# One stationary for w and the decayed q in the gated delta layer, and the next block's q and k scaled ahead of this block's output

## The reference

```python
q = l2norm(heads(q, DK_A)) * (DK_A ** -0.5)
k = l2norm(heads(k, DK_A))
...
qg = q * jnp.exp(gc)[..., None]                 # decayed q
kg = k * jnp.exp(gc[..., -1:] - gc)[..., None]
def step(S, inp):                               # S is 128 x 128 per head
    qg_c, kg_c, u_c, w_c, attn_c, gl_c = inp
    v_new = u_c - jnp.einsum('bhck,bhkv->bhcv', w_c, S)
    o = jnp.einsum('bhck,bhkv->bhcv', qg_c, S) + jnp.einsum('bhij,bhjv->bhiv', attn_c, v_new)
    S = S * gl_c[..., None, None] + jnp.einsum('bhck,bhcv->bhkv', kg_c, v_new)
    return S, o
...
o = rmsnorm(o, g_norm) ; o = o * jax.nn.silu(z)
```

## Time and profile before

| | us |
|---|---|
| median of 3 runs | 4349.92 (4340.74, 4349.92, 4349.94) |
| the profiled execution, its own time | 4347.94 |
| its span | 4346.2 |
| PE busy in the span | 3972.3 (91%) |
| DVE, ACT, POOL busy | 2370.6 (55%), 1386.5 (32%), 843.3 (19%) |

### The profile page before, as it was taken

How to read it: one execution, slowest core, us unless ns; L and a number is a source line. 1 busy time by engine, 2 the same in 40 slices (tenths; PEclk the granted TensorE clock), 3 DMA queues, 4 the chain that set the end, 5 groups by cost and what they waited for, 6 DMA issues and landing times. The chain is left out here.

```text
span 4346.2 us, 58235 instructions
## 1 busy us (share of the span) xinstructions
PE 3972.3 (91%) x22955; PEld 2621.1 (60%) x22955; DVE 2370.6 (55%) x4650; ACT 1386.5 (32%) x2924; POOL 843.3 (19%) x544
## 2 busy tenths in 40 slices
PE   8999999996999999997899999997999999899877
PEld 4555555553455454555888888886656565565544
DVE  4566556652233333332556566662256676778875
ACT  1222222221111111111333333332244454565552
POOL 0344334432122211121222222220000000000000
PEclk9999999997999999998999999996999999999998
DMA  6343334234011110014000000012010100000000
GB/s 245 128 141 112 136 127 141 103 121 150 26 36 36 36 32 27 30 36 151 25 24 23 26 26 26 16 63 79 30 35 18 34 18 23 30 18 18 18 13 17
DMA packets 139772, 259.86 MB, mean 60 GB/s; under 512 B 17205, under 2 KB 64650, under 8 KB 139402
## 3 DMA queue, kind: packets, MB, share of 16 engines
q1 hardware_dynamic: 139530, 256.46, 17.0%
HBM read 217.11 MB, written 39.33 MB: 59 GB/s over the span
## 5 line engine op out<-in xcount | busy, mean ns | idle before, releaser
L459 PE MATMUL e_ps<-arena 128*128 128x386 f32 x1792 | 611.6, 492 | 17.8 <-DVE e_hh L716 7.0
L1082 PE MATMUL o_ps<-arena,o_xT 128*128 128x512 f32 x1280 | 564.4, 594 | 0.8 <-ACT o_xT L1190 0.8
L459 PEld LDWEIGHTS e_ps<-arena 128*128 128x128 f32 x1792 | 331.1, 191 | 249.1 <-issue 32.8
L1082 PEld LDWEIGHTS o_ps<-arena,o_xT 128*128 128x128 f32 x1280 | 239.2, 191 | 279.0 <-issue 278.9
L1612 PE MATMUL d_ps<-hT_in,arena 128*128 128x128 f32 x3072 | 393.3, 283 | 13.4 <-ACT hT_in L1798 11.4
L1612 PEld LDWEIGHTS d_ps<-hT_in,arena 128*128 128x128 f32 x3072 | 360.4, 193 | 29.0 <-ACT hT_in L1798 12.6
L2402 PE MATMUL s_ps<-hT_in,arena 128*128 128x128 f32 x2160 | 257.3, 279 | 6.7 <-PEq L67 6.7
L2402 PEld LDWEIGHTS s_ps<-hT_in,arena 128*128 128x128 f32 x2160 | 253.7, 196 | 10.1 <-issue 9.1
L1171 PE MATMUL o_ps<-o_w_out,o_gt 128*128 128x512 f32 x512 | 225.2, 598 | 4.6 <-ACT o_gt L1247 4.6
L2526 PE MATMUL s_ps<-arena 128*128 128x512 f32 x512 | 228.3, 600 | 0.0
L560 PE MATMUL e_ps<-e_w_out,e_gt 128*128 128x512 f32 x512 | 225.0, 598 | 0.0
(11 more groups left out here) (458 smaller groups left out, 6626.2 us busy)
## 6 DMA issues: line engine op xcount, KB each, us to landing
arena<-l_w_in SPq DMA_DIRECT2D x32, 1040.0 KB, 8.5
xb<-x SPq DMA_DIRECT2D x64, 512.0 KB, 3.4
arena<-l_w_in SPq DMA_DIRECT2D x16, 1544.0 KB, 8.7
arena<-l_w_in SPq DMA_DIRECT2D x16, 1024.0 KB, 8.6
arena<-l_w_in SPq DMA_DIRECT2D x32, 504.0 KB, 7.1
o_scratch<-w_ada SPq DMA_DIRECT2D x16, 768.0 KB
arena<-l_w_in SPq DMA_DIRECT2D x5, 2048.0 KB, 18.9
arena<-w_in SPq DMA_DIRECT2D x5, 2048.0 KB, 14.1
```

Of the source, the lines that this page charges most:

```text
L459: m = pe.matmul(bank[(g + k) % 2][:, 0:N], rows[:, kk * P:(kk + 1) * P], cols[:, kk, :], start=(kk == 0 and k in (0, 1, 4)), stop=(kk == 3 ...
L1082: m = pe.matmul(bank[c % 2][:], xT[:, k * P:(k + 1) * P], W_in[:, k, off:off + 512], start=(k == 0), stop=(k == KT - 1))
```

## The change

1. w transposed and the decayed q of a chunk go into one buffer `wq`, side by side: 64 columns of w and 64 of q for each head. One matmul per head and chunk (four in place of eight per chunk) multiplies S by both. In chunk 0 w has columns 0 to 63, in chunk 1 it has columns 64 to 127, so that w times S lies at the chunk's own rows; the decayed q times S lies at the other half. Chunk 0 goes to bank 7, chunk 1 to bank 2.
2. The output is therefore spread over two banks, with the halves of the partitions exchanged. attn times `vnew` goes there, ScalarE squares it with two instructions of 64 rows, DVE scales it with eight instructions of 64 rows (four before, of 128), the gate z is copied from its bank with the halves exchanged (two instructions of 64 rows for each part, and one for the small columns), and SP stores it with two DMAs.
3. Bank 2 is also where the inverse's products go, so TensorE's wait for the output of the turn before stands in front of the inverse now.
4. On TensorE one piece of filling comes between the first chunk's product and its update, where the product with q stood, and one less behind `turn_qk` (two, not three).
5. On DVE the scaling of q and k of block j stands in front of the output of block i, not behind it.
6. POOL scales q turned with two instructions of half the size. ScalarE waits for `gz` before it copies a new z.

The diff, cut to its core:

```diff
-        qgT = qn
-        wT = sb("wT", [P, 4, P])
+        wq = sb("wq", [P, 2, 4, P])
 ...                                     # sync
-                sp.dma_start(oa_out[bass.ds(b.i * P, P), :], oa[:]).then_inc(oa_stored.sem, 16)
+                for a in (0, DC):
+                    sp.dma_start(oa_out[bass.ds(b.i * P + a, DC), :], oa[DC - a:P - a, :]).then_inc(oa_stored.sem, 16)
 ...                                     # tensor
                 pe.wait_ge(*R_ready.upto(i))
+
+                pe.wait_ge(*oa_ready.before(i))
 ...
-                pe.wait_ge(*oa_ready.before(i))
                 for n in range(2):
 ...
                     for h in range(4):
-                        m = pe.matmul(bank[2][a:a + 64, h * P:(h + 1) * P], wT[:, h, a:a + 64], S[:, h, :], start=True, stop=True)
+                        m = pe.matmul(bank[(7, 2)[n]][:, h * P:(h + 1) * P], wq[:, n, h, :], S[:, h, :],
+                                      start=(h == 0), stop=False, skip_group_check=True)
                     m.then_inc(*wS_made.inc())
-
-                    for h in range(4):
-                        pe.matmul(bank[7][a:a + 64, h * P:(h + 1) * P], qgT[:, h, a:a + 64], S[:, h, :],
-                                  start=(h == 0), stop=False, skip_group_check=True)
+                    if n == 0:
+                        fill()
                     if n and not b.last:
                         turn_v(j)
 ...
                 for h, a in tiles:
-                    m = pe.matmul(bank[7][a:a + DC, h * P:(h + 1) * P], attn[a:a + DC, h, :], vnew[a:a + DC, h, :], start=False,
-                                  stop=True, skip_group_check=True)
+                    m = pe.matmul(bank[2 if a else 7][DC - a:P - a, h * P:(h + 1) * P], attn[a:a + DC, h, :], vnew[a:a + DC, h, :],
+                                  start=False, stop=True, skip_group_check=True)
                 m.then_inc(*o_made.inc())
                 if not b.last:
                     turn_qk(j)
-                    fill(3)
+                    fill(2)
 ...                                     # scalar
-                act.activation(osq[:], by_head[7], ACT.Square).then_inc(*osq_ready.inc())
+                act.activation(osq[DC:P], by_head[7][DC:P], ACT.Square).then_inc(*o.inc())
+                act.activation(osq[0:DC], by_head[2][0:DC], ACT.Square).then_inc(*osq_ready.inc())
 ...
                 if not b.last2:
+                    act.wait_ge(*gz_ready.upto(i))
                     project(b.i + 2, p, 3)
 ...                                     # vector
                 if not b.last:
                     sums_qk(j)
+                    normalise_qk(j)
                 dve.wait_ge(*ro_ready.upto(i))
                 dve.wait_ge(*gz_ready.upto(i))
 
-                dve.wait_ge(oa_stored.sem, 16 * i + 1)
-                for h in range(4):
-                    dve.scalar_tensor_tensor(oa[:, h * P:(h + 1) * P], by_head[7][:, h, :], ro[:, h:h + 1], gz[:, h, :],
-                                             ALU.mult, ALU.mult).then_inc(*(oa_ready if h == 3 else o).inc())
+                dve.wait_ge(oa_stored.sem, 32 * i + 1)
+                for n, a in ((7, DC), (2, 0)):
+                    for h in range(4):
+                        dve.scalar_tensor_tensor(oa[a:a + DC, h * P:(h + 1) * P], by_head[n][a:a + DC, h, :], ro[a:a + DC, h:h + 1],
+                                                 gz[a:a + DC, h, :], ALU.mult, ALU.mult)\
+                           .then_inc(*(oa_ready if n == 2 and h == 3 else o).inc())
                 if not b.last:
-                    for stage in (normalise_qk, copy_kT, mask_products):
+                    for stage in (copy_kT, mask_products):
                         stage(j)
 ...                                     # gpsimd
-                pool.tensor_tensor(qgT[:], qT[:], eG[:], ALU.mult).then_inc(*qg_ready.inc())
+                pool.tensor_tensor(wq[:, 0, :, DC:P], qT[:, :, 0:DC], eG[:, :, 0:DC], ALU.mult).then_inc(*o.inc())
+                pool.tensor_tensor(wq[:, 1, :, 0:DC], qT[:, :, DC:P], eG[:, :, DC:P], ALU.mult).then_inc(*qg_ready.inc())
```

More of the change, by code:

```diff
@@ L1575, in body @@
                 sp.wait_ge(*oa_ready.upto(b.i))
-                sp.dma_start(oa_out[bass.ds(b.i * P, P), :], oa[:]).then_inc(oa_stored.sem, 16)
+                for a in (0, DC):
+                    sp.dma_start(oa_out[bass.ds(b.i * P + a, DC), :], oa[DC - a:P - a, :]).then_inc(oa_stored.sem, 16)
             over_pipeline(sp, body)
-            sp.wait_ge(oa_stored.sem, 16 * BLOCKS + 1)
+            sp.wait_ge(oa_stored.sem, 32 * BLOCKS + 1)
             sp.wait_ge(h_stored.sem, 16 * BLOCKS + 1)
@@ L1804, in project @@
                 else:
-                    act.activation(zba[:, p, (c - 3) * ZH:(c - 2) * ZH], bank[c % 2][:, 0:ZH], ACT.Copy).then_inc(*proj_ready.inc())
+                    n = ZH if c == 3 else 512 - ZH
+                    for a in (0, DC):
+                        act.activation(zba[DC - a:P - a, p, (c - 3) * ZH:(c - 3) * ZH + n], bank[c % 2][a:a + DC, 0:n], ACT.Copy)\
+                           .then_inc(*(proj_ready if c == 3 and a else o).inc())
+                    if c == 4:
+                        act.activation(ba[:, p, :], bank[c % 2][:, n:ZH], ACT.Copy).then_inc(*proj_ready.inc())
             def softplus(i, p):
@@ L1933, in body @@
                 act.wait_ge(*wu_made.upto(i))
-                act.activation(wT[:, :, 0:DC], by_chunk[2], ACT.Copy).then_inc(*wT_ready.inc())
-                act.activation(wT[:, :, DC:P], by_chunk[5], ACT.Copy).then_inc(*wT_ready.inc())
+                act.activation(wq[:, 0, :, 0:DC], by_chunk[2], ACT.Copy).then_inc(*wT_ready.inc())
+                act.activation(wq[:, 1, :, DC:P], by_chunk[5], ACT.Copy).then_inc(*wT_ready.inc())
                 act.activation(u[:], by_head[3], ACT.Copy).then_inc(*u_ready.inc())
@@ L2101, in body @@
                     dve.wait_ge(*wS_made.upto(i, n + 1))
-                    dve.tensor_tensor(vnew[a:a + 64], u[a:a + 64], by_head[2][a:a + 64], ALU.subtract).then_inc(*vnew_ready.inc())
+                    dve.tensor_tensor(vnew[a:a + 64], u[a:a + 64], by_head[(7, 2)[n]][a:a + 64], ALU.subtract).then_inc(*vnew_ready.inc())
                     if not b.last:
```

## The result

| | us |
|---|---|
| before, median of 6 | 4348.99 (4340.74 to 4350.14) |
| after, median of 6 | 4366.67 (4365.66 to 4370.70) |
| ratio | 1.0048, 95% interval 1.0038 to 1.0059 |
| after, the profiled execution: its own time, its span | 4370.70, 4368.9 |

The change makes the kernel slower: 0.48% by the ratio of the runs, 17.7 us (0.41%) between the medians. The two measures differ by less than the width of the interval. The forecast was 4362 (range 4349 to 4380, slower with 0.68).

A forecast was written before the change was run, and what follows sets the result against it. Bound: nearly TensorE's own work, with a chain through DVE and ScalarE ending each turn. 14 turns x 0.8 = 11.2, -1.4, +0.4, clock +2.4: +12.6 on 4347.94 gives 4360.5, median 1.98 higher; forecast 4362, range 4349 to 4380.

The forecast's parts named there:

- turn 14: Turn without filling: -0.77 and -0.54 for update waits, -0.3 of L2036, 0.2 of output uncovered; -1.4 us.
- turn 15: Last turn, no filling: -1.54, then at the open end +0.49 squares, +1.14 output, +0.34 second DMA issue; +0.4 us.
- a term of 0.27: On TensorE, `turn_qk` comes 0.27 us later than before, since one more piece stands in front of it.
- three turns pay 0.8 each: Key products L1666 in slow-clock stretches: 3 turns, from an open 0 to 14, lose some 0.8 us each; +2.4.
- my own sign: Check on the changed trace: forecast right for another reason if the clock is 0.50 in more than half the turns.
- The clock falls in every turn: Rival: all 14 turns lose 0.8 to 2 us to the slow clock, in place of 2.4 altogether; 4371 to 4388; chance 0.13.
- my own case: The forecast's case: 0.45 to 1.15 us a turn and 0 to 6 slow-clock turns, 4354 to 4371; chance 0.60.
- term of 0.2 for changes of half: DVE's output: 0.11 us per change between halves of the rows, twice; output ends at 17.67, not 17.46.
- The rival of cheap instructions on 64 rows: At L2129 on DVE: from 0.15 us each a turn is 0.3 shorter, 4344; even at 0.18 to 0.20; chance 0.19.
- The rival of TensorE's work as the bound: TensorE's saving stays: a turn loses 1.5 us, 14 turns 21, time 4328; chance 0.06.

The follow-up runs named there:

- experiment 1: The changed kernel with k turned copied between the two halves of the output's eight DVE instructions; median 4346.18 us, ratio 0.9997 to the kernel before.
- experiment 6: The kernel before with only the output cut into eight instructions of 64 rows, in the old order; median 4364.59 us, ratio 1.0046.
- experiment 3: The changed kernel with filling as before: no piece behind the first chunk's product, three behind `turn_qk`; median 4351.94 us, ratio 1.0011 to the kernel before.
- experiment 4: The changed kernel with eight unread matmuls ahead of turning q and k and eight ahead of the key products; 4359.30 us, ratio 1.0028 to before.
- experiment 10: The kernel before without the inverse's first filling piece, ScalarE's copy of the third four projection pieces moved behind the squares; 4332.33 us, ratio 0.9966.
- 7: The changed kernel with output split about the copy of k, three pieces behind `turn_qk`, inverse's first piece dropped; 4331.51 us, ratio 0.9965 to before.
- experiment 5: The kernel before with q and k scaled ahead of the output, and ScalarE waiting for `gz` before copying z; 4345.93 us, ratio 0.9997.
- experiment 2: The changed kernel with the output again ahead of scaling q and k on DVE; median 4389.44 us, ratio 1.0098 to the kernel before.

## Why the prediction was right

By its own steps, with t = 0 at the first product (2613.58):

| step | forecast | measured |
|---|---|---|
| joint product, start to start of the next | 0.96 | 0.89 (before 0.93) |
| update 1, product 2 | 2.94, 5.78 | 2.77, 5.72 |
| wait for `vnew`, second chunk | 0.42 | 0.42 |
| `turn_qk` | 9.85 | 9.73 |
| L1657 turns the scaled q, wait | 15.48, 1.2 | 15.42, 1.09 |
| eight of L2129 | 2.2 to 2.4 | 2.32 |
| copy of k turned | 17.67 | 17.65 |
| wait in front of L1666 | 1.7 to 1.9 | 1.86 |
| a turn at the full clock | 58.4 (+0.8) | 58.28 (+0.69) |
| turns 0 to 13, slow clock | +2.4 | +10.3 |
| turn 14 | -1.4 | +2.5 |
| turn 15 | +0.4 | +1.3 |
| sum in the layer, profile on profile | +10.2 +2.4 = +12.6 | +20.0, of it -3.7 ahead of turn 0 |

**The mechanism held, step by step.** The place (the output's eight instructions ahead of the copy of k) is shown by experiment 1, which takes them away from there and gets 1.03 a turn back, and its price by experiment 6: 1.14 for cutting the output alone (there ahead of the scaling, so not the same place). Experiment 3 adds what my sum had as a term of 0.27 only: a piece left behind `turn_qk` would have hidden enough to make the turn shorter than before.

**The clock is the term that was mis-sized,** by a factor of four. I let three turns pay 0.8 each. Nine slow stretches fell into the 14 turns, and eleven turns are longer than 58.28. One stretch costs 10.3 / 9 = 1.1. The products take some 0.6 more (2633.62 - 2631.95 = 1.67 in the turn shown, 1.09 in experiment 4). The piece of L1617 behind them takes 1.0 more, all of it under the wait for `T`. And a wait of 0.3 to 0.55 for the copies of z comes in front of the turning of h (L1598, 2.9 us over 7 turns), at the start of turns that follow a slow piece. I had set that wait at 0, and in the turns at the full clock it is. My reason for three, that the idle stretch is shorter than the one in turn 14, was no reason: all 14 turns have 4.1 us with 1.1 busy there, and in nine of them the clock went to 0.50. By my own sign (over half of the turns at 0.50) the forecast is in part right for another reason. At the full clock the 14 turns would cost 9.7, which alone lies only just over 0.2%. "The clock falls in every turn", which I gave 0.13, is closer to what came than the three turns of my sum. In the changed kernel's profile the loss is about half chain and half clock. The Trainium skill ("TensorE: Matmul & The Clock Gate", section "HAM oscillation — how this bites in real kernels") describes a loop in which a wait for data in every turn makes every turn start at the slow clock. The trace agrees in kind: most turns run their products slow, behind a wait. But no slow stretch begins in five turns with the same waits, so such waits do not always bring it.

**Turn 14 was wrong in sign.** It takes 2.5 more, where I had 1.4 less. Over the kernels above it takes anything from 51.6 to 58.0; the slow stretches fall at other places in each, and no run separates its parts, so the cause stays open. **Turn 15** was sized low at its open end: the output 1.20 longer (2.32 against 1.12, forecast 1.14), the squares 0.61 (3032.18 - 3031.57, forecast 0.49), and the two DMA issues 0.75 (forecast 0.34):

```profile
3036.51 1.09 SPq L1576 DMA_DIRECT2D oa<-d_oa  x2
```

This is the counterpart of the last row. Together 2.56, of which 1.3 remain; by subtraction the rest saved some 1.3, where I had 1.54 for the updates. Both kernels run turn 15 at 0.50 from end to end.

**Ahead of turn 0** 3.7 us were gained that the forecast doesn't have. 1.0 of it comes from layers that are not touched. The other 2.7 came with a shorter stretch at the half clock (3.4 us, before 6.8) where the first blocks are prepared. The seven traces of kernels with the joint product all have the 3.4, and 85.5 to 85.7 us up to the first `T`; the five without it have the 6.8, and 88.2 to 88.4. So this is the change's doing, but by which of its parts, and that the shorter slow stretch is what gains it, was not tested.

**Luck in the total.** The forecast added 12.6 us; turns 0 to 15 took 23.8 more between the two profiles (the slow clock 7.9 above its term, turns 14 and 15 together 4.8, the full-clock turns 1.5 below theirs). That 4362 lies only 5 from 4366.67 is owed in part to the 3.7 gained ahead of turn 0, which I had not seen; the profiled execution of after is also the longest of its six, so that the medians are 5 us closer than the profiles. The bounds of my own case, 4354 to 4371, come out at 4355 and 4370 by their terms; nothing hangs on it.

**The held instruction.** The term of 0.2 for changes of half came out at 0.17 (2631.23 - 2628.98 = 2.25, less the 2 x 1.04 of the earlier trace rows). The rival of cheap instructions on 64 rows falls by the mean of one, taken from the groups of the output in experiment 10 (128 rows) and in 7 (64 rows):

```profile
L2121 DVE SCALAR_TENSOR_TENSOR d_oa<-d_ps,d_ro,d_gz 128x128 f32<-128x128 f32 x56 | 15.8, 344 | 7.0 <-ACT d_ro L1950 7.0
```
```profile
L2130 DVE SCALAR_TENSOR_TENSOR d_oa<-d_ps,d_ro,d_gz 64x128 f32<-64x128 f32 x112 | 32.0, 348 | 0.9
```

344 ns and 348 ns. The rival of TensorE's work as the bound falls too: some 2 us of work went (1.97 by the earlier trace rows, 2.3 between 7 and 10), and the turn became longer.

## What to carry to other kernels

Whoever joins two matmuls should count first what the readers of the joint result pay: half the rows cost DVE the same (348 ns against 344 ns here), so a result laid over two halves doubles each reader, and the order on that engine decides whether this lies in a chain. Work taken off an engine that waits in a chain comes back as waits, and when two of these stand close together the clock may fall as well (in 9 of 14 turns here, in none of experiment 6). Filling should be moved so that idle time is in small pieces, and the same refilling must be given to the old version before the new one is credited. Filling has consumers: when a piece slides to a later place, look where its copy stands in the next engine's queue.

## What the runs showed that I had not expected

- Sixteen matmuls a turn that nobody reads made the changed kernel 7.4 us faster (experiment 4), since they kept the clock at 1.00.
- 128 columns of float32 weights in place of 64 made the product of a chunk no longer: 0.89 from its start to the next instruction, against 0.93.
- Two DMA issues of 64 rows in a row take 1.09 together (0.45 and 0.60), where one of 128 rows took 0.34.
- The order of the DVE instructions is worth nothing with four instructions of 128 rows (experiment 5) and 0.57 a turn with eight of 64 (experiment 2).
- ScalarE's squares on 64 rows by 512 take 0.59 each, as the one on 128 rows (0.60 in the earlier trace rows), and on different halves they start 0.61 apart; the pair of L1855 on 128 rows starts some 0.49 apart.
